# Gate units of the gated MLP: third convolution tap read from the SBUF copy, PSUM bank given back after the copy

## The reference, cut to what matters

```python
h = rms_norm(x, norm2_g)
gate, val = split(h @ ffn_w_up, 2)        # 1024 -> 2 x 3072
gate = causal_dwconv(gate, w, b)          # y[t] = b + w0*g[t-2] + w1*g[t-1] + w2*g[t], per channel
x = x + (gelu(gate) * val) @ ffn_w_down   # 3072 -> 1024
return rms_norm(x, final_norm_g)
```

## Time and profile before

| what | value |
|---|---|
| time, median of 3 runs | 1855.85 us (1855.73 to 1857.02) |
| profiled execution: its time | 1858.44 us |
| its span on core 0, the slowest | 1856.9 us (cores 1851.3 to 1856.9) |
| TensorE matmul / VectorE / ScalarE / GpSimd busy | 95% / 60% / 57% / 28% |
| granted TensorE clock, mean | 0.992 |
| L970, copy of a gate unit | x192, mean 604 ns |
| L974, third tap of a gate unit | x192, mean 783 ns |
| L981, the two other taps | x384, means 785 and 818 ns |

### The profile page before, as it was taken

How to read it: one execution, slowest core, us unless ns; L and a number is a source line. 1 busy time by engine, 2 the same in 40 slices (tenths; PEclk the granted TensorE clock), 3 DMA queues, 4 the chain that set the end, 5 groups by cost and what they waited for, 6 DMA issues and landing times.

```text
span 1856.9 us, 33265 instructions; the slowest of 8 cores (1851.3 to 1856.9 us)
## 1 busy us (share of the span) xinstructions
PE 1755.5 (95%) x9943; PEld 910.1 (49%) x10130; DVE 1113.0 (60%) x2162; ACT 1064.1 (57%) x1832; POOL 524.8 (28%) x694
## 2 busy tenths in 40 slices
PE   9888989999899999999999999999989999899998
PEld 6445445554455544544444544555445554454445
DVE  3875887257851487536882488615884157753653
ACT  4574566447864578734573466635685457842641
POOL 2443343133511244113610334112441122203210
PEclk9999999999999999999999999999999999999999
DMA  9885587976343253434625354432624334244543
GB/s 290 261 236 172 176 270 247 217 180 196 123 156 129 103 199 120 154 133 143 230 95 179 137 182 159 153 131 103 227 104 158 114 109 155 90 159 159 182 142 131
DMA packets 56142, 306.52 MB, mean 165 GB/s; under 512 B 5792, under 2 KB 7968, under 8 KB 32288
## 3 DMA queue, kind: packets, MB, share of 16 engines
q1 hardware_dynamic: 52768, 298.10, 47.9%
q0 software_dynamic: 3200, 6.29, 2.3%
HBM read 266.62 MB, written 44.04 MB: 167 GB/s over the span
## 4 chain that ended last, share of the span: by engine, by line
PE 82%; issue 6%; DVE 5%; ACT 3%; DMA 3%; POOL 1%; DVEq 0%; SPq 0%; ACTq 0%; POOLq 0%
PE pb L765 38%; PE pb L789 18%; PE pb L781 6%; PE pb L1111 6%; PE pb L1145 6%; PE pb L1377 2%; PE pb L773 2%; PE pb L1447 2%; DMA ring<-wd 1%; PE pb L588 1%; ACT PT L1133 1%; DMA tG<-stage 1%; DVE H L626 1%; ACT tG L974 1%; PE pb L914 1%
## 5 line engine op out<-in xcount | busy, mean ns | idle before, releaser
L765 PE MATMUL pb<-H,ring 128*128 128x512 bf16 x3686 | 857.4, 381 | 34.4 <-ACT tG L974 14.3
L765 PEld LDWEIGHTS pb<-H,ring 128*128 128x128 bf16 x3784 | 361.2, 98 | 452.8 <-issue 56.6
L1133 ACT ACTIVATE PT<-pb 128x512 bf16<-128x512 f32 (+3 forms) x640 | 314.7, 532 | 289.8 <-PE pb L1111 125.2
L789 PE MATMUL pb<-aT,ring 128*128 128x512 bf16 (+1 forms) x1568 | 347.2, 369 | 3.4 <-DMA ring<-wd 1.4
L617 POOL TENSOR_TENSOR tN<-tN 128x512 f32<-128x512 f32 x147 | 192.8, 1312 | 534.8 <-ACT tN L608 523.4
L1004 DVE TENSOR_TENSOR xp<-pb,xp 128x512 f32<-128x512 f32 x125 | 86.2, 690 | 302.2 <-PE pb L789 228.1
L789 PEld LDWEIGHTS pb<-aT,ring 128*128 128x128 bf16 x1608 | 153.2, 98 | 154.8 <-issue 4.7
L1111 PE MATMUL pb<-qz,KT 128*128 128x512 bf16 (+3 forms) x627 | 185.0, 348 | 23.3 <-ACT PT L1133 19.1
L608 ACT ACTIVATE tN<-xp 128x512 f32<-128x512 f32 x162 | 101.3, 629 | 179.4 <-DVE xp L1004 156.8
L1145 PE MATMUL pb<-Va,PT 128*128 128x129 bf16 x2176 | 187.6, 220 | 14.4 <-DVE tO L1181 9.4
L991 DVE TENSOR_TENSOR aT<-pb,aT 128x512 bf16<-128x512 f32 x192 | 130.9, 686 | 115.4 <-PE pb L765 106.5
(11 more groups left out here) (107 smaller groups left out, 1647.6 us busy)
## 6 DMA issues: line engine op xcount, KB each, us to landing
ring<-wa SPq DMA_DIRECT2D x128, 1024.0 KB, 4.9
ring<-wd SPq DMA_DIRECT2D x56, 768.0 KB, 4.2
xp<-wa SPq DMA_DIRECT2D x36, 1024.0 KB, 8.5
xp<-x SPq DMA_DIRECT2D x64, 512.0 KB, 8.8
wa<-ring SPq DMA_DIRECT2D x15, 1024.0 KB, 10.6
out<-xp SPq DMA_DIRECT2D x28, 512.0 KB, 6.9
ring<-wd POOLq DMA_DIRECT2D x8, 768.0 KB, 11.5
wd<-ring SPq DMA_DIRECT2D x8, 768.0 KB, 8.3
```

The lines of the kernel that those rows point to most:

```text
L765: last = e.matmul(banks[bank][:], lhsT=rv(r)[:, kk * 512 + c * 128:kk * 512 + (c + 1) * 128], rhs=hd[0][:, kk, :], start=(kk == 0), stop=( ...
L789: last = e.matmul(banks[bank][:, 0:hi - lo], lhsT=rv(r)[:, kk * 128:(kk + 1) * 128], rhs=aT[:, kk, lo:hi], start=(kk == 0), stop=(kk == 23))
L1133: yield o_act(N, lambda e: e.activation(out=PT[:, p, 0:N], in_=banks[bank][:, 0:N], func=AF.Exp), [b_ps[bank]], [b_PT[p]], "exp")
```

## The change

The bank goes back to the pool right behind the copy, ahead of the request for the second buffer. The third tap's ScalarE operation reads the copy in SBUF, `tG[:, gb, 2:514]`, in place of the bank, so its recorded input is the buffer `b_G[gb]` and no longer `b_ps[bank]`. Function, scale, bias and output stay.

```diff
             yield o_act(G, lambda e: e.activation(out=tG[:, gb, 2:514], in_=banks[bank][:], func=AF.Copy),
                         [b_ps[bank]], [b_G[gb]])
+            yield put("bank", bk)
             w = lambda j: pv("fcw", fc * 3 + j, fc * 3 + j + 1)
             ga = yield get("G")
-            yield o_act(G, lambda e: e.activation(out=tG[:, ga, 0:G], in_=banks[bank][:], func=AF.Identity, scale=w(2),
-                                                  bias=pv("fcb", fc, fc + 1)), [b_ps[bank], b_prm], [b_G[ga]])
-            yield put("bank", bk)
+            a_ = o_act(G, lambda e: e.activation(out=tG[:, ga, 0:G], in_=tG[:, gb, 2:514], func=AF.Identity, scale=w(2),
+                                                 bias=pv("fcb", fc, fc + 1)), [b_G[gb], b_prm], [b_G[ga]])
+            yield a_
             yield o_pool(2, lambda e: e.tensor_copy(out=fhalo[:, fc, :], in_=tG[:, gb, 512:514]), [b_G[gb]],
                          [b_fhalo[fc]], dur=0.45)
```

## The result

The changed kernel takes 1869.4* us (1865.9, 1869.4 and 1871.5), the kernel before beside it 1856.16: ratio 1.0066 with an interval of 1.0050 to 1.0083. It is slower by about 12 us. Forecast were 1850.4 us and a gain of 5.4.

The account below looks back on a forecast made before the run. TensorE, busy 95% of 1856.9 us, was taken as the bound. Waits shortened by 7.2 us less 1.8 us of added ScalarE cost gave 5.4 us, so 1855.85 became 1850.4 us; 8-in-10 range 1843.5 to 1860.5, own range 1847 to 1854.

Parts of the forecast that it names:

- One wait, 0.67 us: Behind three units abreast, at 868.99, releasing the bank at the copy lets TensorE start 0.67 us earlier.
- (a) and (b): Seven TensorE waits for the third tap above 0.67 us give 4.7 us; six shorter ones vanish, 2.5 us.
- (c): Waits of 1.91 and 1.90 us at 504.67 and its twin go, but the next wait for VectorE grows: counted 0.
- The clock clause: If the wait at 509.74 grows from 1.45 to 3.4 us, it and its twin lose 3.4 us to lower clock.
- The operation: Third tap reading SBUF takes +0.03 us and starts 0.19 us later behind its copy: at most 42 us of ScalarE.
- What of it reaches TensorE, 1.8 us: Of ScalarE's added time, 1.8 us reaches TensorE, whose scores wait for exps; bounds 0 and 14 us.
- given back: TensorE's next waits for VectorE grow; a third of 7.2 us kept, 1.8 us paid: 1855.3 us, chance 0.27.
- More than shown: New order also cuts waits for exps; all 15.1 us gained less 1.8 us: 1842.6 us, chance 0.15.
- ScalarE the bound: Where late-group attention and gate units run together, ScalarE costs 14 us against 7.2 gained: 1862.7 us, chance 0.16.
- Does not do what it says: TensorE takes something else first; third-tap waits reappear under other names; time as in given back, no chance of its own.
- the signs of being wrong: L991 and L1181 waits up over 4 us; L1133 waits up over 3, ScalarE over 92% busy; very different order.
- the signs of being right: No third-tap waits; copy waits 3 us; three-abreast wait about 0.9 us; third tap about 0.81 us; fillers near 600.

Follow-up runs that it names:

- the kernel with the order kept: Third tap reads the SBUF copy as in the change, but the order, buffers and fillers of the kernel before are replayed: 1852.81 us, ratio 0.9984.
- the other order: Kernel before planned with 0.16 for 0.15 us per step between engines: 1847.97 us, ratio 0.9963; that order replayed with the new source: 1845.17 us, ratio 0.9955.
- its waits filled: Other order with the new source, plus 62 matmuls of ones ahead of long TensorE waits, writing unused attention-bank columns: 1843.35 us, ratio 0.9920, against 1845.17 us without.

## Why the prediction was wrong

Its steps one by one, measured on the kernel with the order kept:

- **One wait, 0.67 us.** Right: 1.56 to 0.90 us.
- **(a) and (b), 7.2 us.** Right: all waits together are 7.0 us shorter in the account. 2.4 us of waits for the copy are left; 3 were forecast.
- **(c), nothing gained at 504, the next wait over 3 us.** Right: 3.54 us.
- **The clock clause.** It stood as an addition to the last rival, 1.7 us at each place, 3.4 together. Its size was right (3.7 measured), its place was not: it belonged in the main sum, which had it at nothing. Over all the half clock took back 4.3 of the 7.0 us (12.9 to 17.2).
- **The operation.** +0.03 us taken, 0.778 to 0.817 us in the median (0.813 in the changed kernel), +0.04 measured; the dependent start +0.19 taken, +0.20 measured (0.10 ahead to 0.10 behind). Right.
- **What of it reaches TensorE, 1.8 us.** Too much: the waits for exps did not grow (19.1 to 17.5 us in that kernel, 18.2 in the changed one).

Net -3.0 us was measured with the order kept and -4.5 in the other order, against -5.4 forecast. The mechanism of one order was right. That -4.5 is near the forecast is no proof of the sum, since no account shows what it is made of.

**The step that failed** is the one that carried this sum over to the changed kernel. The prediction knew that "the order is planned anew", and gave it to a rival that only gains; that "an order so different that its waits no longer stand in the same places" might come stood in the last sentence, without a price and without a chance. That is what happened: with the new source in both, the new order costs 15 us of span over the old (1863.7 to 1848.8): 1.1 us of waits, 10.7 of ones that cover waits, 1.7 of half clock, 1.3 in the rest. Since the ones lie in waits, the new order leaves TensorE some 12 us more to wait. Why the planner's order comes out so is not known.

The rivals: *given back* has the right shape at 504 and 1381, but not its size, since 7.0 us of waits did go. *More than shown* did not come. *ScalarE the bound* had the right sign for a wrong reason: ScalarE is busy for 17.7 of 24 and 28.2 of 35 us in the windows, less than before, and of the three longest waits only the one at 1618 stands behind a full ScalarE. *Does not do what it says* is refuted with the order kept; in the changed kernel the waits for the third tap went, and more time than they had stands in waits under other names and in ones.

Of the signs of being wrong only the last came. TensorE's waits for L991 and L1181 grew by 2.8 us in sum (20.1 to 22.9), those for L1133 did not. Two of the signs of being right were missing: the waits for the copy came to 7.2 us and not 3, and the fillers to 700 records and not "near 600", which by itself said that it was another order.

## What to carry to other kernels

- Where a planner orders the work, a change of one dependence is two changes: what it does in the old order, and a new draw of the order. Here the first is worth -3 to -4.5 us and the second anything over 22. Price the draw, by the spread of orders under nudges that change no instruction, and judge the change with the order held.
- If the order is to be drawn anew anyway, draw several. The fastest here is another order with the new source, 1843.2*, or with its waits filled 1843.35 us, ratio 0.9920 (0.9906 to 0.9934); the two cannot be told apart.
- Ask of each wait that a change makes longer whether the granted clock will fall behind it. Matmuls of ones gained 5 us in two of three kernels where they wrote what nobody waits for, and cost their whole length where they wrote the bank that was awaited.

## What the runs showed of the hardware

On the eight cores of the kernel before, the changed one and the one with the order kept, the granted clock was 1.2 GHz within 4 us behind 54 of 55 waits of TensorE of 3.5 us or more, 35 of 37 of 2.9 to 3.4, 29 of 42 of 2.3 to 2.8 and 3 of 32 of 1.9 to 2.2. The length alone does not decide. With the order kept core 4 stayed at 2.4 GHz behind 3.91 us:

```profile
223.53 1.89 PE L786 MATMUL pb<-H,ring 128*128 128x512 bf16 x8 [3.91 <-DVE aT L1016]
```

And six of its eight cores fell to 1.2 GHz behind a wait of 1.7 us at 476 us, while all eight of the kernel before stayed at 2.4 GHz behind 1.91 us. Taking 20.8 us of waits out of a kernel by work that computes nothing (61.3 to 40.5) made it 5.0 us faster.

Not expected, and only seen: VectorE's L887 takes 0.68 us each at 890 and 1.42 us each at 896, in the changed kernel. What differs beside them is GpSimd, whose tensor operations follow one another almost without a pause from 896.89 on. In turn GpSimd's copy of 3 columns takes 4.43 us while VectorE runs six L887 in a row:

```profile
889.83 4.43 POOL L879 COPY lhalo<-tL 128x3 f32<-128x3 f32 x1 [1.12 <-ACT tL L876]
890.15 4.06 DVE L887 SCALAR_TENSOR_TENSOR tL<-tL,prm 128x512 f32<-128x512 f32 x6
...
896.89 1.54 POOL L617 TENSOR_TENSOR tN<-tN 128x512 f32<-128x512 f32 x1
```

So the 4.70 us at 905 may be two engines in each other's way as much as a queue; this is argued and not shown, since no run here changed one of them alone. The Trainium skill, "GPSIMD Engine Reference", section 1 (Specifications), says that it shares its SBUF interfaces with VectorE and that the two contend where a VectorE instruction has two SBUF inputs; L887 has, and these rows agree.
